# The first norm's token sums from the turned copy: squares on ScalarE, adds on GpSimd, a small product on TensorE

## What is computed

```python
def rms_norm(x, g):
    xf = x.astype(jnp.float32)
    y = xf * lax.rsqrt(jnp.mean(xf * xf, axis=-1, keepdims=True) + EPS)
    return (y * g.astype(jnp.float32)).astype(x.dtype)

for l in range(DEPTH):
    h = rms_norm(x, attn_norm_g[l])
    proj = h @ w_in[l]                       # 1024 -> 4768 columns
    c_q, c_kv, k_rope, gq, gk, gv, pool_in, gate_logits = split_columns(proj, IN_SIZES)
    ...                                      # three branches: MLA, GQA, pooling; gates
    x = x + merged @ w_out[l]
    ...                                      # feed-forward
```

## Time and profile before

| what | value |
|---|---|
| time of the kernel, median of 3 runs | 1470.04 us (1469.83 to 1470.35) |
| the profiled execution's own time | 1469.65 us |
| its span, first to last instruction | 1467.9 us |
| TensorE busy | 1459.9 us, 99% |
| VectorE, ScalarE, GpSimd busy | 75%, 60%, 4% |
| granted clock of TensorE, mean | 0.999 |
| DMA, mean over the span | 175 GB/s |

### The profile page before, as it was taken

The page is one execution under the profiler, slowest core; times in us unless marked ns, Lnnn a source line. Parts: engine busy times, 40 slices in busy tenths (PEclk is TensorE's granted clock), DMA queues, the critical chain, the costliest instruction groups (busy, mean ns, idle before and its releaser), DMA issues.

```text
span 1467.9 us, 20026 instructions
## 1 busy us (share of the span) xinstructions
PE 1459.9 (99%) x7774; PEld 1235.0 (84%) x7774; DVE 1098.2 (75%) x1626; ACT 884.2 (60%) x1341; POOL 56.9 (4%) x69
## 2 busy tenths in 40 slices
PE   9999999999999999999999999999999999999998
PEld 7878888888898778888888888888888898888887
DVE  7897779996578878799956687875467567887446
ACT  6565657775447565677744586764456455766435
POOL 1110000000021000000000001000010000100001
PEclk9999999999999999999999999999999999999999
DMA  8643546666555435556665534656646543566562
GB/s 299 206 145 109 163 143 207 190 196 195 177 165 184 132 115 177 168 189 199 188 191 202 173 101 130 222 189 198 191 158 237 165 128 135 178 193 195 188 192 81
DMA packets 74015, 256.62 MB, mean 175 GB/s; under 512 B 8640, under 2 KB 9920, under 8 KB 73920
## 3 DMA queue, kind: packets, MB, share of 16 engines
q1 hardware_dynamic: 73776, 255.33, 54.5%
q10 hardware_dynamic: 144, 0.00, 0.0%
HBM read 254.25 MB, written 1.05 MB: 174 GB/s over the span
## 4 chain that ended last, share of the span: by engine, by line
PE 94%; DVE 3%; ACT 2%; DMA 0%; issue 0%; POOL 0%; SPq 0%; DVEq 0%; ACTq 0%; POOLq 0%
PE psum L1305 19%; PE psum L1332 18%; PE psum L1336 18%; PE psum L1334 18%; PE psum L1311 10%; PE psum L1261 4%; PE psum L1476 1%; PE psum L1508 1%; DVE w_low L2247 1%; ACT w_high L1727 1%; PE psum L1622 1%; PE psum L1569 1%; PE psum L1654 1%; PE psum L1325 1%; PE psum L1323 1%; PE psum L1326 1%
## 5 line engine op out<-in xcount | busy, mean ns | idle before, releaser
L2247 DVE TENSOR_TENSOR w_low<-w_raw,w_high 128x1024 fp32r<-128x1024 f32 (+2 forms) x482 | 574.2, 1198 | 209.0 <-ACT w_high L1727 207.8
L1727 ACT ACTIVATE w_high<-w_raw 128x1024 fp32r<-128x1024 f32 (+2 forms) x482 | 498.5, 1039 | 252.6 <-PE psum L1336 218.2
L1305 PE MATMUL psum<-x_parts,w_high 128*128 128x512 f32 x992 | 248.8, 393 | 0.0
L1305 PEld LDWEIGHTS psum<-x_parts,w_high 128*128 128x128 f32 x992 | 178.6, 189 | 32.1
L1332 PE MATMUL psum<-w_high,x_parts 128*128 128x512 f32 (+2 forms) x432 | 169.2, 392 | 1.0 <-DVE w_low L2247 1.0
L1336 PE MATMUL psum<-w_high,x_parts 128*128 128x512 f32 (+2 forms) x432 | 163.9, 379 | 0.0
L1334 PE MATMUL psum<-w_low,x_parts 128*128 128x512 f32 (+2 forms) x432 | 163.8, 379 | 0.0
L1311 PEld LDWEIGHTS psum<-x_parts,w_low 128*128 128x128 f32 x992 | 135.3, 190 | 9.7
L1311 PE MATMUL psum<-x_parts,w_low 128*128 128x256 f32 x992 | 138.3, 282 | 0.0
L1332 PE MATMUL psum<-w_high,ff_high 128*128 128x512 f32 x256 | 99.8, 390 | 0.0
L1334 PE MATMUL psum<-w_low,ff_high 128*128 128x512 f32 x256 | 99.6, 389 | 0.0
(11 more groups left out here) (296 smaller groups left out, 2322.2 us busy)
## 6 DMA issues: line engine op xcount, KB each, us to landing
w_raw<-in_weights SPq DMA_DIRECT2D x450, 512.0 KB, 3.7
w_raw<-in_weights SPq DMA_DIRECT2D x16, 384.0 KB, 3.1
w_raw<-in_weights SPq DMA_DIRECT2D x7, 416.0 KB, 3.7
rows<-in_second_rows SPq DMA_DIRECT2D x4, 512.0 KB, 4.9
w_raw<-in_weights SPq DMA_DIRECT2D x6, 256.0 KB, 2.7
scratch<-in_x_turned SPq DMA_DIRECT2D x4, 256.0 KB, 5.0
residual<-in_x SPq DMA_DIRECT2D x2, 512.0 KB, 7.0
dil_masks<-in_consts SPq DMA_DIRECT2D x1, 768.0 KB, 6.2
```

Of the source, the lines that this page charges most:

```text
L1305: eng.matmul(acc[:, f * PANEL:(f + 1) * PANEL], wh[:, j, f * P:(f + 1) * P], parts[:, k, :, :].rearrange("p s n -> p (s n)"), start=k == 0 ...
L1727: act(self.unit_view(self.wh, u), raw, ACT.Copy).then_inc(sem("w_high"), 1)
L2247: tt(self.unit_view(self.wl, u), raw, self.unit_view(self.wh, u), ALU.subtract).then_inc(sem("w_low"), 1)
```

## The change

The token sums are taken from `x_turned`, which is there already. ScalarE squares all of it in two instructions of 128x1024 (`tile_squares`); GpSimd adds the eight tiles down to two by three additions of 128x512 (`mean` of this stage); TensorE sums over the partitions by four float32 products with the column of -0.5 (`token_sums`, into bank 6); VectorE scales them out of PSUM (`rstd`), and GpSimd raises them to -1/2 as before. The load by rows moves to behind unit 27 of the matmuls, and the first adder of the residual waits for it.

```diff
-        self.after(3, lambda: (add("square", g, 0), add("mean", g), self.prefetch(0, 6), add("square", g, 1),
-                               add("rstd", g)))
-        self.after(4, lambda: (add("constants"), add("diag", g)))
+        self.after(2, lambda: (self.prefetch(0, 5), add("tile_squares"), add("mean", g)))
+        self.after(3, lambda: self.prefetch(0, 6))
+        self.after(6, lambda: (add("token_sums"), add("rstd", g), add("constants"), add("diag", g)))
...
         self.after(20, lambda: self.add("load_rest"))
+        self.after(28, lambda: self.add("load_x"))
...
+        self.tile_squares = [by_tile(self.scr[:, (2 + i) * UNIT:(3 + i) * UNIT]) for i in range(2)]
...
-                elif 4 <= n <= 5:
-                    c = slice((n - 4) * PANEL, (n - 3) * PANEL)
-                    eng.dma_start(self.x[:, :, c], src[:, :, c]).then_inc(sem(f"x_loaded{n - 4}"), 16)
...
+            elif kind == "load_x":
+                for half in range(2):
+                    c = slice(half * PANEL, (half + 1) * PANEL)
+                    eng.dma_start(self.x[:, :, c], src[:, :, c]).then_inc(sem("x_loaded"), 16)
...
+            elif kind == "token_sums":
+                q.wait_ge(sem("pool_step"), 1)
+                q.wait_ge(sem("mean_ready"), at("mean", STAGE_MIX[0]))
+                for t in range(TT):
+                    for i in range(2):
+                        d = eng.matmul(bank[6][:, 2 * t:2 * t + 2], self.tile_squares[0][:, i, t * P:(t + 1) * P],
+                                       self.half[:, 0:2], start=i == 0, stop=i == 1, skip_group_check=True)
+                d.then_inc(sem("tokens_summed"), 1)
+                free[6] = (sem("mean_whole"), at("rstd", STAGE_MIX[0]))
...
+            elif kind == "tile_squares":
+                for j in range(2):
+                    q.wait_ge(sem(f"x_arrived{2 * j + 1}"), 16)
+                    act(self.tile_squares[j], self.arriving[:, 4 * j:4 * j + 4, :], ACT.Square
+                        ).then_inc(sem("arrived_high"), 1)
...
+            elif kind == "rstd" and key[0] == STAGE_MIX[0]:
+                q.wait_ge(sem("tokens_summed"), 1)
+                sums = bank[6][:, 0:2 * TT].rearrange("p (t n) -> p t n", n=2)[:, :, 0]
+                ts(self.stat[:, 2:4], sums, -2.0 / D, EPS, ALU.mult, ALU.add).then_inc(sem("mean_whole"), 1)
...
+                if g == STAGE_FFN[0]:
+                    q.wait_ge(sem("x_loaded"), 32)
...
-            if kind == "mean":
+            if kind == "mean" and key[0] == STAGE_MIX[0]:
+                a, b = self.tile_squares
+                for n, part in enumerate((a, b)):
+                    q.wait_ge(sem("arrived_high"), DK + n + 1)
+                    q.step(tt(part[:, 0:2, :], part[:, 0:2, :], part[:, 2:4, :], ALU.add))
+                q.settle()
+                tt(a[:, 0:2, :], a[:, 0:2, :], b[:, 0:2, :], ALU.add).then_inc(sem("mean_ready"), 1)
+
+            elif kind == "mean":
```

More of the change, by code:

```diff
@@ L1061, in x_ready @@
     def x_ready(self, q, g, half):
-        if g == STAGE_MIX[0]:
-            q.wait_ge(self.sem(f"x_loaded{half}"), 16)
-        elif g in (1, 2, 3, 4):
+        if g in (1, 2, 3, 4):
             q.wait_ge(self.sem("x_added"), self.at("residual", g, half))
```

## The result

The changed kernel takes 1474.14 us (median of 7 runs, 1473.38 to 1475.32) against 1470.04 (1469.54 to 1470.35) for the kernel before beside it: 4.1 us more, a ratio of 1.003 with a 95% interval of 1.002 to 1.004. That is slower by more than 0.2%, and above the range of the prediction (1470.0 to 1473.6). The profiled execution took 1474.19 us, with a span of 1472.4.

A forecast was written before the change was run, and what follows sets the result against it. TensorE's work was taken to bound the kernel. Eight passes (0.87 us) and a stall (0.70), with 0 for load 3, the load by rows and later waits, made +1.6 us: 1471.6 on the median, range 1470.0 to 1473.6.

The forecast's parts named there:

- What bounds the kernel: TensorE, busy 1459.9 of 1467.9 us, sets the time; at most 0.85 us could be won, at the start.
- Part 1: At the start, the load by rows leaves: load 3 unmoved, gain 0 to 0.16 us, taken as 0; new place costs 0.
- Part 2: ScalarE's squares ahead of unit 6's copy: its low part ends at 16.9, 0.3 us by itself, covered behind token_sums.
- Part 3: token_sums on TensorE: four float32 products make eight new passes, 0.87 us (0.43 if columns set the pace).
- Part 4: TensorE at token_sums waits for GpSimd's three additions, 1.1 us each: a stall of 0.7 us.
- rival B: GpSimd's additions and VectorE's low parts for units 5 and 6 block each other: stall 2.6 us, 1473.5; chance 0.12.
- the sum: Whole kernel: load 3 at 0, eight passes 0.87, stall 0.70, load by rows and later waits 0: +1.6 us.
- What would show it: List of signs in the profile: right, a token_sums wait of about 0.7 us; wrong, one over 2 us, among others.
- Part 5: Behind the start: take_c 2.7 us later, `row` covered by 0.6 to 1.6 us, heads' turn with 1.1 us left.
- Rivals A: GpSimd's additions take about 0.69 us, done at 16.2; passes of 0.43 to 0.87 remain: 1470.5 to 1471.0; chance 0.18.
- C: Chain behind take_c moves 2 us more than 2.7; TensorE waits about 1 us at the heads' turn: 1472.6; chance 0.12.
- D: At the start load 3 lands earlier, the 0.85 us gap closes, passes cost 0.43: 1469.6; chance 0.10.

## Why the prediction was wrong

**What bounds the kernel: right.** TensorE's work sets the end, and a shift at 17 us is a shift of the end: 4.5 us at the start became 4.5 us of span. No gain was possible, and none came.

**Part 1, load 3 and the load by rows, cost 0: right as far as it was measured.** Unit 4 started at 12.19 in the changed kernel's profile and between 11.78 and 12.41 in seven others with the load there, around the 12.01 of before. That moves by more than the 0 to 0.16 us in question. No wait appeared where the load went.

**Part 2, the low part of unit 6 hidden behind token_sums: right only while something stands in front of it.** It ended at 17.37, not 16.9, because it waited for GpSimd; with the products moved away TensorE waited 0.44 us for it.

**Part 3, eight passes at 0.87 us: right.** They took 0.88 in the changed kernel and 0.81 with the additions on VectorE, 0.10 to 0.11 us for a pass of two columns, as for one of 128 columns (0.87 for eight). The weights set the pace, not the columns.

**Part 4, a stall of 0.7 us: this step failed.** It was 1.81. My sum "with two inputs read in turn, 512 elements make 0.19 + 2 x 0.46 = 1.1 us" had a slip in it, since my own 1 ns for an element makes 0.19 + 2 x 0.51 = 1.2; measured were 1.30 for the first two and 2.13 for the third. Of the 1.1 us too little, 0.8 is the third addition's wait for VectorE (2.13 less 1.30); the rest is the additions' own length, less the 0.18 by which TensorE came later. The overlap that I took for free, GpSimd adding while VectorE subtracts, isn't free. That is rival B's mechanism, which I gave 0.12. I held against it that VectorE's subtraction at 79.55 ran untouched inside a GpSimd instruction with two inputs. The row was true and the conclusion wrong: an instruction on 16 elements says nothing of one on 512. Why that one left VectorE alone wasn't tested. B's own price, a stall of 2.6 us, assumed a slow first use as well, which did not come. On this the Trainium skill was nearer: by its ratio (GPSIMD Engine Reference, elementwise cycle accounting) the addition was estimated at 1.36 us, measured 1.30; and its rule of the shared port pair (SBUF — State Buffer, who interferes with whom) holds in both kernels where both engines read two long inputs. For the powers of 16 elements and for the multiplications with one long input, beside which VectorE lost 0.4 us at most and not a whole instruction, the measurements differ from it.

**The clock: a term that the sum didn't have, and the second step that failed.** It cost 1.6 us, the difference between the changed kernel (+4.1) and the filled wait (+2.5), and the 1.57 by which unit 6 is quicker there. I had worked out a standstill of 0.7 to 2.6 us and passes of two columns behind it, and priced them by length alone. "What would show it" named a wait over 2 us and an addition that starts only as VectorE's subtraction ends, and not this. (The third addition starts inside the subtraction in the trace and is long instead.) Without the clock term and with the measured stall the sum is 0.18 + 1.81 + 0.88 = 2.9, 1472.9 on the median, inside the range: it is the clock that takes the result out of it.

**Part 5, later waits: right.** take_c came 1.96 us later (2.7 allowed), `row` did not wait, and the turns waited no longer than before. Rivals A, C and D did not come.

What the runs did not settle: when the clock falls behind the same standstill, and why the half clock then lasts 3 us in one profile and nearly 7 in another (1473.38 to 1475.32 for the changed kernel, 1472.41 to 1475.71 with the load by rows in its old place); why the powers of 16 elements left VectorE alone; and what GpSimd and VectorE share when GpSimd reads one input.

## What to carry to other kernels

Where one engine is busy for 99%, an idea that moves work from engines with room onto it (here sums from ScalarE and VectorE to eight TensorE passes) starts with a loss that is easily priced, 0.88 us, and what it makes that engine wait for is the larger part. Before helping out with GpSimd, look at what VectorE does in the same microseconds: here two long instructions with two inputs each didn't run side by side. And a wait of TensorE, or a stretch of products with very few columns, is to be priced with what the clock may do behind it, and both should be kept apart by full work.

## What the runs showed of the hardware

The granted clock of TensorE fell to 0.50 behind 1.8 us of standstill and 0.9 us of two-column passes in a row, in another profile 0.3 us into those passes, and behind 4.4 us of such passes alone with TensorE never idle. In the profiled runs it stayed at 1.00 behind 1.7 us of standstill alone and behind 0.8 us of passes alone, with full matmuls on the other side, and behind 24 passes (2.6 us); three of the nine timed runs of that kernel look like a fall. At 0.50 a 512-wide matmul follows its neighbour by 0.43 us, at 1.00 by 0.23.

GpSimd's addition of 128x512 in float32 takes 1.30 us alone, 2.13 to 2.16 when it starts while VectorE's subtraction of 128x1024 is under way; the subtraction takes 1.22 alone and 2.28 to 2.32 when it starts with such an addition ahead of it. The addition that was under way when a subtraction started kept its 1.30. Beside one-input multiplications of 128x512 on GpSimd the subtraction takes 1.23 to 1.65.
